# A state-space branch in six parts beside a stream of dense tiles, and nine throwaway products in each norm

## The reference, cut to what matters

```
h = rms(x, g_norm)
q, k, v, f, gf, u, gs, qm, gm, gl = split(h @ w_in)      # one wide projection
s5  = state_space(u)           # 48 groups, 16 inputs and 64 complex states each:
                               #   s[t] = a*s[t-1] + B u[t];  y[t] = Re(C s[t])
y   = gelu(y + d*u);  y_s5 = y * sigmoid(y @ w_glu + b_glu) * silu(gs)
y_fox = causal attention of q, k, v with a forget gate from f, then gated by gf
y_mem = attention of qm on a memory, gated by gm
x   = rms(x + merge(y_fox, y_s5, y_mem) @ w_out, g_final)
two layers of attention and MLP follow, each with two norms
```

## Time and profile before

| | us |
|---|---|
| median of 3 runs | 2686.73 (2686.25 to 2688.16) |
| the profiled execution, its own time | 2691.79 |
| its span, first to last instruction | 2689.7 |
| TensorE busy | 2392.1 (89%) |
| VectorE busy | 1425.8 (53%) |
| GpSimd busy | 1113.0 (41%) |
| ScalarE busy | 578.6 (22%) |

### The profile page before, as it was taken

The page is one execution under the profiler, slowest core; times in us unless marked ns, Lnnn a source line. Parts: engine busy times, 40 slices in busy tenths (PEclk is TensorE's granted clock), DMA queues, the critical chain, the costliest instruction groups (busy, mean ns, idle before and its releaser), DMA issues.

```text
span 2689.7 us, 30450 instructions
## 1 busy us (share of the span) xinstructions
PE 2392.1 (89%) x12619; PEld 1907.2 (71%) x12619; DVE 1425.8 (53%) x1716; ACT 578.6 (22%) x1157; POOL 1113.0 (41%) x672
## 2 busy tenths in 40 slices
PE   3576699879999995999999799997999999799998
PEld 2465378567766674997766588886997775688887
DVE  4966221442334376655537876666755546773351
ACT  1122211522222222114430343310113440110000
POOL 2310075314233342562305466665464213566663
PEclk7777699889999997999999899998999999899999
DMA  5222262034243352221104365543222103233321
GB/s 158 70 50 41 85 229 79 1 118 141 75 153 126 125 180 90 95 92 63 32 17 150 102 201 174 188 148 99 95 95 75 48 17 110 79 96 106 96 94 47
DMA packets 267556, 271.39 MB, mean 101 GB/s; under 512 B 27980, under 2 KB 252944, under 8 KB 267292
## 3 DMA queue, kind: packets, MB, share of 16 engines
q1 hardware_dynamic: 226148, 234.44, 27.3%
q10 hardware_dynamic: 41272, 35.01, 4.7%
HBM read 253.15 MB, written 13.13 MB: 99 GB/s over the span
## 4 chain that ended last, share of the span: by engine, by line
PE 65%; DVE 6%; ACT 1%; issue 1%; ACTq 0%; DMA 0%; POOL 0%; DVEq 0%
PE ps L430 41%; PE ps L1789 10%; PE ps L518 6%; PE ps L745 2%; PE ps L788 2%; PE ps L764 1%; DVE ps L852 1%; DVE normed L639 1%; DVE ada_acc L343 1%; DVE hT_low L629 1%; PE ps L774 1%; DVE root L634 1%; PE ps L1885 1%; PE ps L618 1%; PE ps L356 0%
## 5 line engine op out<-in xcount | busy, mean ns | idle before, releaser
L222 POOL TENSOR_SCALAR ring_high<-ring 128x1024 fp32r<-128x1024 f32 x302 | 332.3, 1100 | 1461.4 <-DMA ring<-in_w_in_dram 463.4
L224 POOL TENSOR_TENSOR ring_low<-ring,ring_high 128x1024 fp32r<-128x1024 f32 x302 | 751.7, 2489 | 25.2
L430 PE MATMUL ps<-hT_high,ring_high 128*128 128x512 f32 x968 | 392.9, 406 | 36.1 <-issue 16.0
L430 PE MATMUL ps<-hT_low,ring_high 128*128 128x512 f32 x968 | 381.6, 394 | 0.0
L430 PE MATMUL ps<-hT_high,ring_low 128*128 128x512 f32 x968 | 381.2, 394 | 0.0
L343 DVE TENSOR_REDUCE ada_acc<-ring 128x256 f32<-128x2048 f32 x48 | 188.7, 3932 | 113.4 <-ACT ring L330 113.2
L430 PEld LDWEIGHTS ps<-hT_high,ring_high 128*128 128x128 f32 x968 | 184.5, 191 | 85.3 <-issue 23.1
L1789 PE MATMUL ps<-ring_high,hT_high 128*128 128x256 f32 x768 | 222.9, 290 | 20.4 <-DVE hT_low L629 20.4
L1789 PE MATMUL ps<-ring_high,hT_low 128*128 128x256 f32 x768 | 220.2, 287 | 0.0
L1789 PE MATMUL ps<-ring_low,hT_high 128*128 128x256 f32 x768 | 220.1, 287 | 0.0
L430 PEld LDWEIGHTS ps<-hT_high,ring_low 128*128 128x128 f32 x968 | 184.6, 191 | 39.8
(11 more groups left out here) (342 smaller groups left out, 4114.2 us busy)
## 6 DMA issues: line engine op xcount, KB each, us to landing
ring<-in_w_in_dram SPq DMA_DIRECT2D x75, 1024.0 KB, 5.3
ring<-in_w_ff_dram SPq DMA_DIRECT2D x64, 1024.0 KB, 5.4
ring<-in_w_ada_dram SPq DMA_DIRECT2D x48, 1024.0 KB, 7.2
ring<-in_w_out_dram SPq DMA_DIRECT2D x12, 1024.0 KB, 6.5
scratch_x<-xT ACTq DMA_DIRECT2D x3, 2048.0 KB, 7.1
xT<-scratch_x ACTq DMA_DIRECT2D x3, 2048.0 KB, 8.7
ring<-in_w_mem_kv_dram SPq DMA_DIRECT2D x4, 1024.0 KB, 5.1
ring<-in_w_branch_a_dram SPq DMA_DIRECT2D x8, 512.0 KB, 5.8
```

The costliest lines, as they stand in the source:

```text
L222: nc.gpsimd.tensor_scalar(hi, raw, 1.0, 1.0, ALU.mult, ALU.mult).then_inc(hi_done.sem, 1)
L224: nc.gpsimd.tensor_tensor(lo, raw, hi.bitcast(F32), ALU.subtract).then_inc(lo_done.sem, 1)
L430: ins = nc.tensor.matmul(out[0:rows, bank, cols[0]:cols[1]], lhsT, rhs, start=start, stop=stop)
```

## The change

The branch's thirds are replaced by six parts of 8 groups, and all its work is put between products of one `Stream` of 37 tiles: u (6), gs (6), q (6), k (6), f (1), v (12), 888 products in two PSUM banks. The first tile starts with the norm's first block. Numbers fix how many stream products stand ahead of each step: 264 ahead of the first transposes, 300 ahead of the first Toeplitz products, then 66 for each part, of which 24 ahead of the next part's transposes and 54 ahead of its Toeplitz products. Since the slots of the attention's operands are in use, q, k and v are stored to DRAM by ScalarE (`also`) and loaded back behind the stream; q and k pass through four staging tiles. ScalarE, not VectorE, now copies the Toeplitz block. The loads of U and y and the stores of y move from ScalarE's queue to SyncE's, as turns ahead of a slab in `load_weights`, each with a wait for the part's output (for parts 0 to 5 ahead of slabs 9, 11, 12, 13, 15 and 16, with u's first slab as 0). The order of the slabs follows the stream. The forget rows are worked out near the stream's end. The glu's first products wait for each Gelu by itself; its ScalarE step has one tanh more and its VectorE step one product more (the gate's silu). In `rms_stage` TensorE issues nine float32 products of 384 columns, whose result nobody reads, behind the sums, in each norm whose result is split (five of seven).

```diff
-G3 = 16
+G6 = 8
+PARTS = G5 // G6
...
+        for turn in K.sync_turns.get(i, ()):
+            turn(sp)
...
-    for i in range(3):
-        add(f"glu_g{i}", w, dm, O_GS, 768, part=i)
+    add("gs", w, dm, O_GS, 768)
+    add("q", w, dm, O_Q, 768)
+    add("k", w, dm, O_K, 768)
+    add("f", w, dm, O_F, SLAB_W)
+    add("v", w, dm, O_V, 768)
     for i in range(3):
         add(f"glu_z{i}", T["w_glu"][0], (0, 768), 0, 768, False, part=i)
     ada(0)
-    add("f", w, dm, O_F, SLAB_W)
-    add("q", w, dm, O_Q, 768)
-    add("k", w, dm, O_K, 768)
-    add("v", w, dm, O_V, 768)
...
+            if n == 0 and j % 3 == 0 and self.arriving is not None:
+                pe.wait_ge(self.arriving[0].sem, self.arriving[1] + j // 3 + 1)
...
+            if pair:
+                for _ in range(9):
+                    nc.tensor.matmul(K.ps[:, 1, 0:3 * P], K.ident, K.const[:, 0:3 * P], start=True, stop=True)
...
+    tiles = []
+    for name in ("u", "gs", "q", "k"):
+        tiles += column_tiles(K, K.first[name], 6, KD, K.hT)
+    tiles += [[m[:5] + ((K.first["f"], 2),) + m[6:] for m in t] for t in column_tiles(K, K.first["f"], 1, KD, K.hT)]
+    for i in range(3):
+        tiles += token_tiles(K, K.first["v"] + i, K.hT)
+    U_N, GS_N, Q_N, K_N, F_N, V_N = 0, 6, 12, 18, 24, 25
...
+    stream = Stream(K, tiles, [6 + n % 2 for n in range(len(tiles))], take, arriving, also)
+    END = 24 * len(tiles)
+    START, W_MADE = 264, 300
+    turn_at = [(START if n == 0 else W_MADE + 66 * (n - 1) + 24) for n in range(PARTS)]
+    pad_at = [(W_MADE if n == 0 else W_MADE + 66 * (n - 1) + 54) for n in range(PARTS)]
+    out_at = [W_MADE + 66 * (n + 1) for n in range(4)] + [660, 720]
+    turn_at[5], pad_at[5] = 588, 630
...
+    def load_u(sp, n):
+        for r in range(CH):
+            sp.dma_start(U[n % 2][r * H5:(r + 1) * H5, :, :], su_g[:, n * G6:(n + 1) * G6, CH - 1 - r, :]
+                         ).then_inc(u_back[n % 2].sem, 16)
+    def store_y(sp, n):
+        sp.wait_ge(y_copied.sem, n + 1)
+        for r in range(CH):
+            sp.dma_start(sy_g[:, n * G6:(n + 1) * G6, r, :], Y[r * H5:(r + 1) * H5, :, :]).then_inc(y_out[n % 2].sem, 16)
+    def load_y(sp, n):
+        sp.wait_ge(y_out[n % 2].sem, 16 * CH * (n // 2 + 1))
+        if n >= 2:
+            sp.wait_ge(d_done.sem, n - 1)
+        sp.dma_start(yP[:, n, :], K.scratch_y[n * P:(n + 1) * P, :]).then_inc(y_back[n % 2].sem, 16)
+        sp.dma_start(uT[n % 2][:, :], K.scratch_u[n * P:(n + 1) * P, :]).then_inc(y_back[n % 2].sem, 16)
+    def first_turn(sp):
+        sp.wait_ge(us.sem, 16)
+        load_u(sp, 0)
+        load_u(sp, 1)
+    def next_turn(sp, n):
+        sp.wait_ge(y_made.sem, n + 1)
+        if n + 2 < PARTS:
+            load_u(sp, n + 2)
+        if n >= 1:
+            load_y(sp, n - 1)
+        store_y(sp, n)
+    def spread_forget(sp):
+        sp.wait_ge(sm.sem, 1)
+        sp.dma_start(K.scratch_f, fw[:, 4, :]).then_inc(fr.sem, 16)
+        sp.dma_start(causal[:, :], T["const_causal"]).then_inc(fr.sem, 16)
+        sp.wait_ge(fr.sem, 32)
+        rows = K.scratch_f.rearrange("(o h) n -> o (h n)", o=1).broadcast_to([P, FOX_H * SEQ])
+        sp.dma_start(forget[:, :, :].rearrange("p h n -> p (h n)"), rows).then_inc(qb.sem, 16)
+    slab0 = K.first["u"]
+    K.sync_turns[slab0 + 6] = [first_turn]
+    slab_at = lambda x: slab0 + (x // 48 if x < 600 else 13 + (x - 600) // 96)
+    for n in range(PARTS):
+        K.sync_turns.setdefault(max(slab_at(out_at[n]) + 2, slab0 + 7), []).append(lambda sp, n=n: next_turn(sp, n))
+    K.sync_turns.setdefault(K.first["glu_z0"], []).append(lambda sp: load_y(sp, PARTS - 1))
+    K.sync_turns.setdefault(K.first["glu_z2"] + 1, []).append(spread_forget)
...
+            stream.feed(pe, 48)
...
+            stream.feed(pe, 72)
+            pe.wait_ge(ready.sem, 1)
             for i in range(2):
-                ins = nc.tensor.matmul(K.ps[:, 5 + i, 0:384], K.swap,
-                                       C1[:, 24 * i:24 * i + 24, :], start=True, stop=True)
+                ins = nc.tensor.matmul(ps[:, i, 0:384], K.swap, C1[:, 24 * i:24 * i + 24, :], start=True, stop=True)
             ins.then_inc(turned.sem, 1)
+            def turn_part(n):
+                stream.feed(pe, turn_at[n])
+                pe.wait_ge(bk_made.sem, n + 1)
+                if n >= 1:
+                    pe.wait_ge(bkT_copied.sem, n)
+                for g in range(G6):
+                    ins = nc.tensor.transpose(ps[:, 2 + g // 4, (g % 4) * P:(g % 4 + 1) * P], Bk[:, g, :, :], K.ident)
+                ins.then_inc(bk_turned.sem, 1)
+            def pad_part(n):
+                stream.feed(pe, pad_at[n])
+                pe.wait_ge(w_made.sem, n + 1)
+                if n >= 1:
+                    pe.wait_ge(pad_copied.sem, n)
+                for g in range(G6):
+                    ins = nc.tensor.matmul(ps[0:H5, g // 4, (g % 4) * P:(g % 4 + 1) * P], bb1[:, n * G6 + g, :],
+                                           W[n % 2][:, g, 0:CH, :], start=True, stop=True)
+                ins.then_inc(pad_made.sem, 1)
+            turn_part(0)
+            pad_part(0)
+            for n in range(PARTS):
+                pe.wait_ge(bkT_copied.sem, n + 1)
+                pe.wait_ge(u_back[n % 2].sem, 16 * CH * (n // 2 + 1))
+                if n >= 1:
+                    pe.wait_ge(scan_made.sem, n)
+                for g in range(G6):
+                    ins = nc.tensor.matmul(ps[:, 4, g * NC5:(g + 1) * NC5], BkT[:, g, :], U[n % 2][:, g, :],
+                                           start=True, stop=True)
+                ins.then_inc(drive_made.sem, 1)
+                if n + 1 < PARTS:
+                    turn_part(n + 1)
+                    pad_part(n + 1)
+                stream.feed(pe, out_at[n])
+                pe.wait_ge(state_made.sem, n + 1)
+                pe.wait_ge(laid.sem, 16 * CH * (n + 1))
+                if n >= 1:
+                    pe.wait_ge(y_copied.sem, n)
+                for g in range(G6):
+                    out = ps[:, 5, g * NC5:(g + 1) * NC5]
+                    nc.tensor.matmul(out, TT5[:, g, :], U[n % 2][:, g, :], start=True, stop=False)
+                    ins = nc.tensor.matmul(out, W[n % 2][:, g, 1:CH + 1, :], H[:, g, :], start=False, stop=True)
+                ins.then_inc(y_made.sem, 1)
+            stream.feed(pe, END)
...
+            stream.take(e, START - 24)
+            e.wait_ge(ready.sem, 3)
+            nc.scalar.activation(tB[:, :, :], tE[:, :, :], ACT.Sin).then_inc(acted.sem, 1)
+            nc.scalar.activation(tC[:, :, :], tA[:, :, :], ACT.Sin).then_inc(acted.sem, 1)
...
+            copy_turned(0)
+            make_sines(0)
+            for n in range(PARTS):
+                e.wait_ge(drive_made.sem, n + 1)
+                if n >= 1:
+                    e.wait_ge(state_made.sem, n)
+                swapped(ps[:, 4, :].rearrange("p (g c) -> p g c", g=G6), drive_swapped)
+                lay_toeplitz(n)
+                if n + 1 < PARTS:
+                    copy_turned(n + 1)
+                    make_sines(n + 1)
+                e.wait_ge(scan_made.sem, n + 1)
+                swapped(Gs[:, :, :], scan_swapped)
+                stream.take(e, pad_at[n + 1] if n + 1 < PARTS else out_at[n] - 24)
+                e.wait_ge(y_made.sem, n + 1)
+                if n >= 1:
+                    e.wait_ge(y_out[(n - 1) % 2].sem, 16 * CH * ((n - 1) // 2 + 1))
+                nc.scalar.activation(Y[:, :, :], ps[:, 5, :].rearrange("p (g c) -> p g c", g=G6), ACT.Copy
+                                     ).then_inc(y_copied.sem, 1)
+                stream.take(e, out_at[n])
...
+            drive_table(0)
+            angle_table(0)
+            v.memset(pad[:, :, 0:112], 0.0).then_inc(K.sig("pad_cleared").sem, 1)
+            out_table(0)
+            for n in range(PARTS):
+                co, si = cosj[n % 2][:, :, :], sinj[n % 2]
+                drive = ps[:, 4, :].rearrange("p (g c) -> p g c", g=G6)
+                if n + 1 < PARTS:
+                    drive_table(n + 1)
+                e.wait_ge(sines.sem, 2 * (n + 1))
+                step(v.tensor_tensor(co, half[:, :, :], half[:, :, :], ALU.mult))
+                step(v.tensor_scalar(co, co, -2.0, 1.0, ALU.mult, ALU.add))
+                if n + 1 < PARTS:
+                    angle_table(n + 1)
+                e.wait_ge(drive_swapped.sem, n + 1)
+                step(v.tensor_tensor(tmp[:, :, :], X[:, :, :], si, ALU.mult))
+                step(v.tensor_tensor(X[:, :, :], drive, co, ALU.mult))
+                step(v.tensor_tensor(tmp[:, :, :], tmp[:, :, :], X[:, :, :], ALU.add))
+                flat = lambda x: x[:, :, :].rearrange("p g c -> p (g c)")
+                v.tensor_tensor_scan(flat(Gs), flat(rho), flat(tmp), 0.0, ALU.mult, ALU.add).then_inc(scan_made.sem, 1)
+                if n + 1 < PARTS:
+                    e.wait_ge(scan_made.sem, n + 1)
+                    out_table(n + 1)
```

(14 more changed lines are left out.)

556 lines of the change are left out of this document (245 added, 311 removed).

## The result

The changed kernel takes **2620.6 us** (median of 4 runs, 2619.0 to 2622.4); the kernel before, timed beside it, 2687.4 us (4 runs, 2686.3 to 2693.9). The ratio is 0.9747, 95% interval 0.973 to 0.9764: 66.8 us less. The prediction was 2615 us, range 2583 to 2658, and faster. The profiled execution has a span of 2618.3 us at a mean granted clock of 0.960 of TensorE; before it was 2689.7 at 0.933.

The account below looks back on a forecast made before the run. The branch's VectorE, ScalarE and DMA chain was taken as the bound up to 308 us, TensorE from 355.7 to 458.4. Attention 70.4 us earlier plus 1 from the norms: 2686.7 - 71.4 = 2615 us, range 2583 to 2658.

Parts of the forecast that it names:

- What bounds the kernel, and the overlay: Before the attention: the branch's chain bounds up to 308 us, TensorE from 355.7 to 458.4; overlaying them gains 70.4 us.
- Start: Up to the first part's products: TensorE waits 17 us for Bk, ready at 131.5 us; W is ready at 144.1.
- What GpSimd costs VectorE: Beside GpSimd's weight splits, VectorE loses 2.7 us per half; up to 3.8 by the port lock rule.
- One of six parts: Each part takes 28.0 us, paced by VectorE; TensorE needs 24.4 at most and waits some 4 before the Toeplitz products.
- The weights behind SyncE's turns: At v's first slab, behind output 4's turn: TensorE stops 11 us, the chain loses 7.5, output 5 comes at 297.1.
- Output 6: Last part: drive 1.9 us, VectorE and ScalarE without tables 8.2, output 3.8; it ends at 311.0.
- The tail of the stream: After the sixth output: 168 products of 0.121 us and some 3 us for ScalarE's logarithm and Gelu, ending at 334.3.
- Behind the stream: Gated linear unit: 31 us and a tail of 5.0 + 0.7, to 371.0; then 15.4 us waiting for x, to 386.4.
- The sum: The steps up to the attention put its start at 388.0 instead of 458.4 us, 70.4 us less.
- The nine products: In the norms: throwaway products gain at most 1 to 1.5 us in each of two, taken as 1 us less in all.
- TensorE pacing the parts: Rival for the parts: collisions fall into VectorE's waits, period 24.4 us, no loss at v's first slab; 2589 us, chance 0.22.
- The rival of the clock: Rival for the parts: TensorE's clock drops, 48.8 us of its work per part instead of 24.4; 2740 us, chance 0.06.

Follow-up runs that it names:

- e7: The changed kernel with GpSimd making the low half of each weight half of q, k, f and v twice: 2654.1 us, ratio 0.9876.
- e3: The changed kernel with SyncE's turn for the fourth part one weight slab later, behind the first slab of v: 2613.5 us, ratio 0.9722.
- e4: The changed kernel with four of ScalarE's eight issues in the last part moved behind the swap and the copies: 2626.8 us, ratio 0.9768.
- e8: The changed kernel with the last part's Toeplitz matrix laid by SyncE, its accumulators copied earlier by ScalarE: 2619.1 us, ratio 0.9751.
- e6: The changed kernel with the wait for x's return moved from the attention's start to the merge: 2614.9 us, ratio 0.9727.
- e11: The changed kernel with GpSimd subtracting only 16 of 128 columns for the low halves of q, k, f and v: 2599.5 us, ratio 0.9679.

## Why the prediction was right, point by point

- **What bounds the kernel, and the overlay.** Right. The branch's chain and the dense tiles now run over each other, and the attention's first product moved by 61.5 us where the sum had 70.4.
- **Start.** Right. TensorE waited 16.9 us for Bk (17 predicted), and the transposes started at 132.1 with Bk predicted at 131.5. W allowed the Toeplitz products at 142.7 (144.1).
- **What GpSimd costs VectorE.** Right in the mechanism, too small in the size: 2.7 us a half by the working, 3.8 where VectorE is the bound (e7's step to output 3), 3.3 to 3.5 by the place of output 4 over all steps. I had taken it from one window of 27 us in which five halves met 25 operations.
- **One of six parts.** The period is (263.8 - 178.3) / 3 = 28.5 us where 28.0 was predicted, and output 4 ended at 263.8 (261.6). The mean came out by luck, since it hides 23.4, 34.4 and 27.7, and VectorE paced only the second. SyncE's turn for part 1 held the next slab so long that GpSimd stood still for 34 us; the step with few splits (two halves, in its last 8 us) ran at TensorE's period of 23.3 (24.4 at most predicted), and the splits came together in the next one. In the third step TensorE was full at a clock of 0.85: its first 8.1 us ran at the lower level, which costs 4.1, and 27.7 less 4.1 is TensorE's period again. With 2.75 halves at 3.3 to 3.5 us every step paced by VectorE would have been 30. In the second trace of the change output 4 ended at 261.4. TensorE's waits for W, predicted at some 4 us in each, were 6.0, 0, 7.2 and 0.
- **The weights behind SyncE's turns.** Right: 13.3 us for 11, at the slab named, with the turn of 10.3 us taken as 8. Without the stop the step is 7.7 us shorter (e3), where the chain was said to lose 7.5. Output 5 took 39.0 us behind output 4, where 35.5 was predicted.
- **Output 6.** Wrong, and this is the largest miss: 20.3 us instead of 13.9. The step that failed is "ScalarE: ... in an order in which each swap comes before VectorE asks for it". In the last part VectorE has no tables of a next part to make, so it asks for the swap 3.7 us before ScalarE is through its eight issues, and TensorE's banks wait with it. TensorE stops for 5.15 us and then runs 5.2 us at a clock of 0.50, which costs 2.6 more. e4 and e8 show it: with four issues moved the stop is 2.3 us, and with all eight off ScalarE's queue the step takes 16.4 us. The 2.5 us that are left over 13.9 hold the stop of 2.1 us that stays.
- **The tail of the stream.** 20.0 us instead of 23.3: ScalarE's logarithm and Gelu cost TensorE nothing there.
- **Behind the stream.** The unit took 31.1 us of TensorE (31), its end 7.2 instead of 5.7, since a last row of VectorE met GpSimd (2.98 us for 1.05). The new wait was there, 15.0 us with 15.4 taken for it, and x ended it, as e6 shows.
- **The sum.** 2.2 (output 4) + 3.5 (output 5) + 6.4 (output 6) - 3.3 (tail) + 1.5 (unit) - 0.4 - 1.1 (x, and the step to the attention) = 8.8, against the 8.9 by which 396.9 is later than 388.0.
- **The nine products.** "1 us less" can't be told from the nothing that was measured.
- **The rivals.** TensorE pacing the parts was true for two of the three steps between outputs 1 and 4, one of them at a clock of 0.85, and in e11 for all but short waits for ScalarE. The rival of the clock was priced for a clock that stays down, and that did not come: behind 144 us the windows show means of 0.82 to 1.00. But it was not idle either. Behind the stops of 6.0, 7.2, 13.3 and 5.2 us TensorE ran 3.3 to 5.2 us at 0.50 each time, and from 233.9 to 244.2 us it did so though its only wait in the ten us ahead was one of 1.0. In e4 the clock fell within a stop of 2.8 us. So my reading, that a wait of 4 us in each part is just short of what brings the clock down, did not come out: in these traces the length of the last wait alone did not decide it.

The time of 2620.6 is 5.6 us above the forecast of 2615. In the traces the attention came 8.9 us later than the sum has it, and the rest is the stretch behind it, read above. That the time is nearer to the forecast than the attention is, is luck.

## What to carry to other kernels

A wait of TensorE is not free room if what fills it makes another engine work: here the filler products make GpSimd split weights, and each us of that put off the output by 0.82 to 0.87 us, and by nearly a whole one where VectorE was full. Read a period step by step before taking its mean as a success: 23.4, 34.4 and 27.7 us had three reasons. When stages are laid over each other, walk through each in-order queue and each wait at a stage's entry once more, above all in the last turns of the loop, where an engine lacks the neighbour's work that covered its waits; three such places were worth 15 us. Where runs of the same code scatter by more than an edit is worth, compare the start of a stage behind the edit rather than the whole time.

## What was not expected of the hardware

- What GpSimd's work cost was nearly the same in both directions: the fourth output moved by 0.87 us for each of 28.9 us added and by 0.82 for each of 28.6 taken away. In the step in which VectorE was full it lost 0.96 us for each us (e7). A one-input row that began within a subtraction took 2.50 us against 0.43 for the same form, and ended 0.3 us behind it.
- A stop can cost twice: behind waits of 2.3 and 2.8 us with 3.1 us of products between them, the 32 short products of an output ran at a granted clock of 0.50 and took 7.07 us instead of 3.7. The clock also fell where TensorE was at work, at 233.9 us in the changed kernel, 2.5 us behind a wait of 1.0 us.
- Keeping TensorE busy in a norm held its clock at the upper level (1.00 against 0.50 from 44 to 48 us), and the time did not change (ratio 1.0002, 0.9994 to 1.0011), since VectorE's blocks set the pace.
- The stretch behind the attention, with the same instructions but for one wait and the nine products, took 2220 to 2231 us from run to run.
